# Last neighbourhood group: stored rows split one step earlier, output matmuls spread over more slots

## What is computed

```
def hybrid_layer(x, g, w_in, w_out, lq1, lk1, lq2, lk2, subln_g, rpb, lam_init):
    h = rms_norm(x, g)
    z = jnp.einsum('bsd,de->bse', h, w_in)
    qd, kd, vd, qn, kn, vn, gate = jnp.split(z, cuts, axis=-1)
    ...
    o_da = diff_attention(qd, kd, vd, lam, lam_init, subln_g)
    o_na = neighbourhood_attention(qn, kn, vn, rpb)
    o = jnp.concatenate([o_da, o_na], axis=-1) * jax.nn.silu(gate)
    return x + jnp.einsum('bse,ed->bsd', o, w_out)
```

## Time and profile before

| | before |
|---|---|
| median of 3 runs | 1527.42 us (1525.89 to 1529.27) |
| the profiled execution | 1521.68 us |
| its span | 1519.9 us |
| TensorE busy | 1452.2 us (96%) |
| VectorE busy | 907.8 us (60%) |
| ScalarE busy | 698.8 us (46%) |
| GpSimd busy | 508.6 us (33%) |
| mean granted TensorE clock | 0.988 of full |

### The profile page before, as it was taken

One profiled execution on the slowest core, in us unless ns is written; L12 is line 12 of the kernel. 1 busy time (PEld: TensorE's weight loads), 2 busy tenths in 40 slices (PEclk: granted clock), 3 DMA queues, 4 the chain that ended last, 5 costly groups with the idle time before them and its releaser, 6 DMA issues. The chain is left out here.

```text
span 1519.9 us, 24890 instructions
## 1 busy us (share of the span) xinstructions
PE 1452.2 (96%) x8288; PEld 1187.2 (78%) x8288; DVE 907.8 (60%) x1892; ACT 698.8 (46%) x1338; POOL 508.6 (33%) x498
## 2 busy tenths in 40 slices
PE   7899999999999999889999999999999999997994
PEld 6687887878787878678887878788878888886874
DVE  6467676776656565663436766777665555557323
ACT  5345554554544444542515555545554444455330
POOL 2233333243423232302643242423342323231261
PEclk9999999999999999999999999999999999999997
DMA  6500100012111201301210100001112111121012
GB/s 200 118 29 22 48 21 35 35 35 55 40 52 42 59 35 59 132 15 42 69 42 29 36 35 35 21 28 41 53 35 61 42 52 41 52 80 73 32 53 111
DMA packets 39249, 79.45 MB, mean 52 GB/s; under 512 B 18832, under 2 KB 18832, under 8 KB 39184
## 3 DMA queue, kind: packets, MB, share of 16 engines
q1 hardware_dynamic: 39184, 78.60, 15.9%
HBM read 66.57 MB, written 15.96 MB: 54 GB/s over the span
## 5 line engine op out<-in xcount | busy, mean ns | idle before, releaser
L884 PE MATMUL proj<-h_hi,w_hi 128*128 128x512 f32 x1184 | 502.0, 424 | 22.9 <-DVE h_lo L1197 10.3
L886 PE MATMUL proj<-h_hi,w_lo 128*128 128x512 f32 x1184 | 467.6, 395 | 0.0
L885 PE MATMUL proj<-h_lo,w_hi 128*128 128x512 f32 x1184 | 464.2, 392 | 0.0
L884 PEld LDWEIGHTS proj<-h_hi,w_hi 128*128 128x128 f32 x1184 | 223.4, 189 | 97.9 <-issue 51.1
L886 PEld LDWEIGHTS proj<-h_hi,w_lo 128*128 128x128 f32 x1184 | 223.0, 188 | 51.7
L885 PEld LDWEIGHTS proj<-h_lo,w_hi 128*128 128x128 f32 x1184 | 224.6, 190 | 34.5
L1288 DVE CUSTOM_DVE_ANT_0 prob<-scores,inner 128x1024 f32<-128x1024 f32 (+1 forms) x192 | 204.3, 1064 | 50.0 <-PE scores L920 47.2
L1296 DVE TENSOR_TENSOR pt_lo<-turn,pt_hi 128x512 fp32r<-128x512 f32 (+1 forms) x208 | 138.9, 668 | 143.8 <-ACT pt_hi L750 143.5
L750 ACT ACTIVATE pt_hi<-turn 128x512 fp32r<-128x512 f32 (+1 forms) x208 | 120.8, 581 | 225.9 <-PE turn L977 225.9
L558 POOL TENSOR_TENSOR w_lo<-w_raw,w_hi 128x1024 fp32r<-128x1024 f32 x78 | 188.8, 2420 | 106.0 <-ACT w_hi L708 105.9
L776 ACT ACTIVATE prob<-prob,nm,escale_now 128x1024 f32<-128x1024 f32 x128 | 158.1, 1235 | 0.4 <-DVE nm L1292 0.4
(11 more groups left out here) (159 smaller groups left out, 2224.1 us busy)
## 6 DMA issues: line engine op xcount, KB each, us to landing
w_raw<-chunks SPq DMA_DIRECT2D x81, 512.0 KB, 3.2
mixed_dram<-gate SPq DMA_DIRECT2D x28, 256.0 KB, 2.1
edge<-bias_dram SPq DMA_DIRECT2D x32, 224.0 KB, 3.8
h_lo<-mixed_dram SPq DMA_DIRECT2D x14, 512.0 KB, 8.2
xt<-x_t SPq DMA_DIRECT2D x8, 512.0 KB, 9.3
bias_dram<-bias_rows SPq DMA_DIRECT2D x16, 240.0 KB, 5.8
out_t<-prob SPq DMA_DIRECT2D x6, 512.0 KB, 3.0
out_t<-gate SPq DMA_DIRECT2D x2, 512.0 KB, 3.0
```

The costliest lines, as they stand in the source:

```text
L884: pe.matmul(dst, a_hi, b_hi, start=start, stop=False)
L885: pe.matmul(dst, a_hi, b_lo, start=False, stop=False)
L886: return pe.matmul(dst, a_lo, b_hi, start=False, stop=stop)
```

## The change

Three tables get other numbers; no instruction is added or taken away.

```diff
-    LAST_CHUNKS = {2: 1, 6: 2, 7: 3, 8: 4}
-    TAKEN = {2: [0, 1], 3: [2, 3], 4: [4, 5], 5: [6]}
+    LAST_CHUNKS = {2: 1, 5: 2, 7: 3, 8: 4}
+    TAKEN = {1: [0, 1], 2: [2, 3], 3: [4, 5], 4: [6]}
...
-    LAST_FILL = {1: [], 2: [], 3: [[], both([0]), both([1])], 4: [both([2]), [], both([3])],
-                 5: [both([4]), [], both([5])], 6: [both([6]), [(2, range(0, 3))], [(2, range(3, 7))]],
-                 7: [[(3, range(0, 3))], [(3, range(3, 7)), (4, range(0, 2))], [(4, range(2, 7))]],
-                 8: [[(5, range(0, 4))], [(5, range(4, 7))], [(6, most)], [(7, most)]]}
+    LAST_FILL = {1: [], 2: [[], [], both([0, 1])], 3: [[], both([2]), both([3])], 4: [[], both([4]), both([5])],
+                 5: [both([6]), [(2, range(0, 2))], [(2, range(2, 7))]],
+                 6: [[(3, range(0, 2))], [(3, range(2, 5))], [(3, range(5, 7)), (4, range(0, 2))]],
+                 7: [[(4, range(2, 4))], [(4, range(4, 7))], [(5, range(0, 5))]],
+                 8: [[(5, range(5, 7)), (6, range(0, 2))], [(6, range(2, 7))], [(7, range(0, 5))], [(7, range(5, 7))]]}
```

## The result

The changed kernel takes **1535.14 us** (median; 1533.48 to 1537.47), the kernel before 1527.42. The ratio is **1.0052 [1.0036, 1.0068]**: 7.9 us slower, with an interval of 5.5 to 10.4 us.

What follows compares the result with a forecast made beforehand. TensorE's idle time and clock were taken to bound the kernel. Idle time 2.7, clock 1.7 and contention 0.6 made 5.0 us a layer, 10.0 in all, on 1527.42: 1537.4 us, range 1529.5 to some 1542.

Steps and rivals of the forecast that it cites:

- step 2, later shift less four triples: VectorE's first shift in step 2 comes 4.1 us later, four triples cover 2.8 us: +1.3 us idle a layer.
- copy beside GpSimd: VectorE's bias copy in step 1 meets GpSimd's gate product: 0.6 us a layer for all contention there, between 0 and 1.9.
- step 3: Nothing gained: the 2.21 us wait for VectorE's split, slowed beside GpSimd's chunk 1, stays.
- step 4: Wait for a row stays in kind; most of the 0.67 us at the weighted sum goes: -0.6 us a layer.
- step 5: The 2.09 us wait becomes about 1.5 us, now for the addition of piece 0: -0.6 us a layer.
- step 6: Its 0.60 us of idle time, a wait for the addition of piece 0, goes: -0.6 us a layer.
- piece 8, for chunk 4: With two triples left behind the last weighted sum, piece 8 waits for GpSimd's chunk 4: +3.2 us a layer.
- clock behind it: TensorE's clock falls after the new wait before piece 8: 1.7 us a layer, bounds 0 and 1.7.
- The one with the same waits, without the fall and without contention: Rival: the forecast's waits, but no clock fall and no contention: +5.4 us, 1532.8 us; chance 0.27.
- The faster one, in which TensorE's waits go in full: Rival: TensorE's 8.5 us of waits go, only the 3.2 us stall is left: -5.3 us a layer, 1516.8; chance 0.06.
- That of no change: Rival: no measurable change, the wait before piece 8 made good elsewhere, some 1530 us and below; chance 0.15.

Runs made afterwards that it cites:

- second execution: Either kernel profiled once more, unchanged: the kernel before 1523.88 us, the changed kernel 1532.15 us.
- the kernel with step 8's cover kept: The changed kernel, but step 8 keeps all seven triples of piece 7 behind the last weighted sum: 1521.94 us, ratio 0.9979.

## Why the prediction was right

1537.4 us was forecast for 1535.14, and 0.65% for 0.52. By its steps, a layer, with the waits of layer 0 at full clock (see step 4 below):

| step of the prediction | forecast, us | measured, us |
|---|---|---|
| step 2, later shift less four triples | +1.3 | +1.65, with the copy |
| copy beside GpSimd | +0.6 | (in the line above) |
| step 3 | 0 | 0 |
| step 4 | -0.6 | -1.0 |
| step 5 | -0.6 | -0.7 |
| step 6 | -0.6 | -0.5 |
| piece 6, for chunk 3 | none | +0.3 |
| piece 8, for chunk 4 | +3.2 | +3.07 |
| clock behind it | +1.7 | +1.7 in 7 of 8 cases, 1.5 in the mean |
| sum | +5.0 | +4.3 |

Twice 4.3 is 8.6 us, against 7.9 measured, with an interval of 5.5 to 10.4. This sum is softer than it looks. With the waits as they stand in the two first profiles, low clock and all, the steps up to 6 make +0.8 us and not -0.5, and the whole 11.2 us. That the forecast came within 2.3 us is in part luck: the copy was priced too low and the wait before piece 6 left out, while step 4's gain and what the four triples cover were taken too small.

**Step 8** was right in its mechanism, place and size, and both of its conditions were met: the idle time is not given back in the late pieces, and the clock falls behind it. Removing the wait in two ways, by cover and by an earlier rounding, and putting it alone into the kernel before, show it as the cause.

**Step 1 and step 2.** ScalarE began its copies at 633.34, the two in 1.99 us, with no wait for a transfer. The shift was forecast 4.1 us late without the copy's price and 4.7 with the 0.6 taken; it was 4.9. The four triples cover more of it than forecast: they run in two pairs with a wait ahead of each, from 635.78 to 637.38 and from 639.20 to 640.86, which makes the 7.80 - 4.54 = 3.3 us by which TensorE's busy time in step 2 rose, for 2.8 forecast. TensorE waits for rows 0 and 1 (1.82 us twice), then 0.54 and 0.22 us, 4.40 in all for 2.75: +1.65. The working had both rows ready before VectorE reached the split that TensorE needs. They were, but TensorE needs the first row sooner than that, so the wait at the reciprocals' transposes split up into three.

**The copy** was the unknown with the bounds 0 and 1.3 us, and it came near the upper one: 0.75 became 1.84 us, +1.1. GpSimd's product began at 635.20 and ended at 636.78; the copy began at 635.55 and ended at 637.39. The rule of the Trainium skill ("GPSIMD Engine Reference", section "Key points"), by which GpSimd contends with instructions "in a 2-port perf mode or with two SBUF inputs", was left open for this copy in the forecast. The trace shows that the copy, with one fp32 input, contends; whether it ran in such a mode no run here shows. The row that I had taken as the nearest one, the split of 2.60 us, told the mechanism rightly: VectorE ends after GpSimd does. To halve it was the mistake.

**Step 3** was right: 2.22 us for 2.21, with a split of 2.60 us beside chunk 1. That chunk 1 is its cause was argued only; moving the chunk showed it, in either kernel.

**Step 4** is the term that was mis-sized. The forecast read 0.73 + 0.67 us from an execution in which the clock was low there, and took 0.6 off. Where the clock was full ahead of it, before waits 2.27 + 0.68 = 2.95 us in step 4. The changed kernel waits 1.69 us for the row; where the clock then stays full, as in layer 0 of its second execution, the weighted sum waits another 0.22:

```profile
656.49 0.38 PE L1012 MATMUL mix<-pt_hi,v_hl 128*128 128x256 f32 x1 [0.22 <-DVE pt_lo L1297]
```

So the gain is 2.95 - 1.91 = 1.0 us. The low clock was in the rows, since 0.91 stands beside that step, but I used it for a price of its own and not to mend the wait. For the same reason the forecast held that little good comes of the filling: -0.5 us up to step 6, and +0.1 with the copy. By the waits at full clock it is some -0.55 us with the copy (+1.65 - 1.0 - 0.7 - 0.5). No single execution has full clock in all of these steps, so this is worked out and not measured. What is measured is the kernel with step 8's cover kept: 3.2 us faster in all, with an interval of 1.1 to 5.3, of which these waits explain 1.1.

**Steps 5 and 6** were right, with the new wait for the addition of piece 0 at 1.40 us, forecast at 1.5.

**Missed:** the 0.27 us before piece 6. Chunk 3, which is made at the end of step 7, is subtracted from 692.77 to 695.16, and piece 6 now starts in slot 0 of step 8. It is the fault of piece 8 in small. I had checked the cover of one chunk and not of each.

**The rivals.** The one with the same waits, without the fall and without contention (+5.4 us, 1532.8) is 2.3 us off, just as near as the forecast, so the time alone doesn't tell the two apart. The traces do: both costs were there, in 7 of 8 cases and in every copy, and step 4 gave a part of them back. The faster one, in which TensorE's waits go in full, was wrong: 9.7 us of waits are still there in steps 2 to 5, and the shift is late by 4.9 us. That of no change is excluded by the interval.

**The two profiled executions** lie 15.8 us apart. The stretch is 4.58 + 3.50 = 8.1 us longer, and the clock behind piece 8 costs 2 x 1.7 = 3.4. Two more low clocks stand in a place that the change doesn't touch, some 1.7 us each. Before and now, at 402 us, and now at 1146:

```profile
402.00:404.00 2.00, 2.00 (x13) 1.66 (x12) 1.37 (x7) 1.03 (x2) 1.92 (x2) 1.00 0.85 240
```

```profile
402.00:404.00 2.00, 2.00 (x7) 1.41 (x6) 1.77 (x11) 0.38 (x1) 1.43 (x1) 0.53 0.58 156
...
1146.00:1148.00 2.00, 2.00 (x7) 1.46 (x6) 1.63 (x9) 0.25 (x1) 1.50 (x1) 0.56 0.38 136
```

Together that is 14.9 us. Other profiles, the second one of the kernel before among them (1136 to 1140 us), have such falls there in one layer or in both, so they belong to the execution and not to the change. The two second executions agree: the stretch takes 88.06 and 88.55 us for 84.45 and 86.69, which with 3.4 for the clock makes 8.9 us, and they lie 8.3 apart.

**Open.** What decides whether a wait of 1.7 to 2.5 us lowers the clock in a given execution stayed open, and so did the reason for the other 2.1 us of the gain in the kernel with the cover kept.

## What to carry to other kernels

Work that is moved forward to fill waits is taken from somewhere: for each slot that loses work, look up what was made ready beside it (here a chunk of weights whose time was hidden by exactly those triples) and redo that sum for every such product. An engine's wait that is read beside a low clock has to be restated at full clock before anything is subtracted from it. And a filler that needs another operation of the engine that sets the pace buys TensorE's idle time with that engine's time: here two splits of 1.22 us and a longer copy for 3.3 us of triples, and by the waits some 0.5 us a layer are left of it after all is counted.

## What was not expected of the hardware

- A VectorE copy with one fp32 input of 128x1152 took 1.84 us for 0.75 while GpSimd ran an operation with two inputs. The delay goes both ways: GpSimd's product took 1.58 us for 1.27 when VectorE's split was already running.
- GpSimd's operation with one input (`gate_tanh`, 1.49 us) ran beside VectorE's split with two, and the split took 1.22 us, as without it:

```profile
633.62 1.49 POOL L589 TENSOR_SCALAR gate_tanh<-gate_tanh 128x512 f32<-128x512 f32 x1 [1.62 <-ACT gate_tanh L736]
635.20 1.58 POOL L591 TENSOR_TENSOR gate<-gate,gate_tanh 128x512 f32<-128x512 f32 x1
```

- The same code had the clock full behind a wait in one execution and low in the next: behind the 2.5 us wait of step 2 in layer 0 it is 1.00 in the first, and 0.62 from 634 to 636 us in the second. With 3.07 us of waiting it fell in 7 of 8 cases, and behind 1.69 us in step 4 of the changed kernel (0.84 over 10.56 us) too. Each fall costs some 1.7 us, as much as most of the waits themselves, and gives a part back only where another wait follows.
